# Loading the first modulation tiles into a place of their own, in one queue in the order of need

## The reference, cut to what matters

```python
xc = ctx
for l in range(DEPTH):
    mod = jax.nn.silu(c) @ w_mod[l] + b_mod[l]
    mod_c = jax.nn.silu(c_ctx) @ w_mod[l] + b_mod[l]
    sh1, sc1, g1, sh2, sc2, g2 = jnp.split(mod[:, None, :], 6, axis=-1)
    ...
    h = x * (1 + sc1) + sh1
    hc = xc * (1 + sc1c) + sh1c
    y, yc = _token_mixers(h, hc, w_in[l], ...)
```

## Time and profile before

| | |
|---|---|
| median of 3 runs | 3222.01 us (3219.78 to 3222.47) |
| the profiled execution | 3220.32 us, span of its instructions 3219.0 us |
| granted TensorE clock, mean | 0.966 of full |
| busy: PE, DVE, ACT, POOL | 94%, 44%, 33%, 10% |
| loads from HBM | 294.29 MB, 92 GB/s over the span |

### The profile page before, as it was taken

The page is one execution under the profiler, slowest core; times in us unless marked ns, Lnnn a source line. Parts: engine busy times, 40 slices in busy tenths (PEclk is TensorE's granted clock), DMA queues, the critical chain, the costliest instruction groups (busy, mean ns, idle before and its releaser), DMA issues.

```text
span 3219.0 us, 41567 instructions
## 1 busy us (share of the span) xinstructions
PE 3019.1 (94%) x17128; PEld 2308.4 (72%) x17128; DVE 1418.2 (44%) x2184; ACT 1072.9 (33%) x1807; POOL 313.1 (10%) x334
## 2 busy tenths in 40 slices
PE   5989999999999988999999998997889999899998
PEld 3766657788888866766667776775567888678886
DVE  2556542423233345654444445536734444344443
ACT  3235441412122242553422335212533323342222
POOL 1012220300000030221201002000310000110000
PEclk7999999999999999999999999998989999889999
DMA  6313134222212122103343322422322232222322
GB/s 236 94 58 105 34 119 150 86 99 85 66 60 65 58 77 69 60 14 127 134 150 98 103 87 79 165 94 92 99 85 92 94 96 92 67 66 92 98 92 79
DMA packets 83876, 299.08 MB, mean 93 GB/s; under 512 B 9479, under 2 KB 11783, under 8 KB 83432
## 3 DMA queue, kind: packets, MB, share of 16 engines
q1 hardware_dynamic: 79200, 286.30, 27.2%
q10 hardware_dynamic: 4488, 10.12, 0.9%
HBM read 294.29 MB, written 2.10 MB: 92 GB/s over the span
## 4 chain that ended last, share of the span: by engine, by line
PE 87%; DVE 5%; ACT 4%; issue 2%; DMA 1%; POOL 1%; ACTq 0%; DVEq 0%; POOLq 0%
PE bank L592 42%; PE bank L596 21%; PE bank L1013 4%; PE bank L455 3%; PE bank L1030 3%; PE bank L1074 2%; PE bank L2682 2%; PE bank L1828 1%; PE bank L1566 1%; DMA t<-in_mod 1%; PE bank L1450 1%; PE bank L1022 1%; ACT t L1288 1%; ACT t L843 1%; ACT t L1112 1%
## 5 line engine op out<-in xcount | busy, mean ns | idle before, releaser
L592 PE MATMUL bank<-t 128*128 128x512 f32 (+1 forms) x6432 | 1757.3, 374 | 26.5 <-DVE t L2326 11.1
L592 PEld LDWEIGHTS bank<-t 128*128 128x128 f32 x6432 | 1113.0, 189 | 297.1 <-issue 69.1
L596 PE MATMUL bank<-t 128*128 128x512 f32 (+1 forms) x3216 | 1070.7, 372 | 5.9 <-POOL t L852 5.7
L596 PEld LDWEIGHTS bank<-t 128*128 128x128 f32 x3216 | 556.8, 189 | 127.4 <-POOL t L852 12.0
L486 ACT ACTIVATE t<-t 128x1024 fp32r<-128x1024 f32 x350 | 366.3, 1050 | 558.4 <-PE bank L596 497.5
L496 DVE TENSOR_TENSOR t<-t 128x1024 fp32r<-128x1024 f32 x350 | 430.5, 1234 | 262.4 <-ACT t L486 258.8
L609 DVE SCALAR_TENSOR_TENSOR t<-bank,t 128x512 f32<-128x512 f32 x192 | 129.8, 693 | 511.0 <-PE bank L596 484.2
L933 DVE TENSOR_TENSOR t<-t 128x512 f32<-128x512 f32 (+1 forms) x128 | 98.4, 769 | 335.8 <-ACT t L913 335.8
L913 ACT ACTIVATE t<-bank 128x512 f32<-128x512 f32 (+1 forms) x128 | 83.3, 651 | 418.7 <-PE bank L596 418.7
L1214 POOL TENSOR_SCALAR t<-t 128x768 f32<-128x768 f32 (+3 forms) x160 | 125.7, 788 | 576.3 <-DVE t L1182 576.3
L455 PE MATMUL bank<-t 128*32 128x256 f32 x1536 | 128.9, 414 | 33.7 <-DMA t<-in_mod 23.5
(11 more groups left out here) (289 smaller groups left out, 2281.4 us busy)
## 6 DMA issues: line engine op xcount, KB each, us to landing
t<-in_mod SPq DMA_DIRECT2D x192, 512.0 KB, 4.3
t<-in_l0fc SPq DMA_DIRECT2D x64, 512.0 KB, 3.5
t<-in_l1fc SPq DMA_DIRECT2D x64, 512.0 KB, 3.5
t<-in_s0fc SPq DMA_DIRECT2D x64, 512.0 KB, 3.5
t<-in_s1fc SPq DMA_DIRECT2D x64, 512.0 KB, 3.5
t<-in_mixin SPq DMA_DIRECT2D x24, 512.0 KB, 3.5
t<-in_l0in SPq DMA_DIRECT2D x12, 512.0 KB, 3.6
t<-in_l1in SPq DMA_DIRECT2D x12, 512.0 KB, 3.5
```

The source lines that it names most:

```text
L592: pe.matmul(acc.ap[:, o:o + m], w[:, ws], Hh[:, k, o:o + m], start=k == 0 and w is hi, stop=False)
L596: ins = pe.matmul(acc.ap[:, o:o + m], hi[:, ws], Hl[:, k, o:o + m], start=False, stop=k == NK - 1)
```

## The change

The first 16 modulation tiles get a buffer of their own, `early`, 64 KB in each partition. It is allocated and given back before `mixer_memory` is called, so it lies on the bytes of the first mixer's buffers (`cqh` to `F` and the start of `Hh`), which are written only after `mod_at(0, 1)`. None of the 16 loads waits for PE. The four loads of x move from ACT's queue to SP's and lose their waits. SP's first entries are written out by hand: modulation tiles 0 to 12, dense tiles 0 and 1, the first quarter of x, modulation tiles 13 to 15, the other three quarters of x, dense tiles 2 and 3. From there on the sorted order is as before, with modulation tiles 16 to 18 first. ACT and DVE split two dense tiles, not three, before they make h, and the third after it.

```diff
--- before.py
+++ after.py
@@ -247,7 +247,7 @@
 def first_order(t, l):
     name = f"l{l}"
-    t.tile((name + "in", 3))
+    t.tile((name + "in", 3), 0 if l else 1)
     t.tile((name + "in", 4), 1)
     for i in (5, 6, 7, 8, 0, 1, 2, 9):
         t.fill(1, l + 1)
@@ -364,7 +364,7 @@
     XTt = sb(ctx, [P, NK, T])
     XT = [XTt[:, k, :] for k in range(NK)]
-    NR, NS, NM = 4, 3, 3
+    NR, NS, NM, NE = 4, 3, 3, 16
     modw = sb(ctx, [P, NM, 1024])
     whi = sb(ctx, [P, NS, 1024], F32R)
@@ -418,23 +418,44 @@
     def sp_tiles():
-        first = seq.place[seq.mod_keys[10]]
-        tiles = [(seq.freed_at(seq.keys[i - NR]) if i >= NR else first, seq.place[key], key)
-                 for i, key in enumerate(seq.keys)]
-        mods = [(seq.place[seq.mod_keys[i - NM]] if i >= NM else -1, seq.place[key], key)
-                for i, key in enumerate(seq.mod_keys)]
-        for _, _, key in sorted(tiles + mods, key=lambda x: x[0:2]):
-            if key in seq.index:
-                i = seq.index[key]
-                if i >= NR:
-                    SPQ.wait_ge(*at("pe_tile", i - NR))
-                sp.dma_start(raw[:, i % NR, :], din[key[0]][key[1]]).then_inc(*up(f"tile_in{i % NR}", i, 16))
-            else:
-                i = seq.mods[key]
-                if i >= NM:
-                    SPQ.wait_ge(*at("pe_mod", i - NM))
-                sp.dma_start(modw[:, i % NM, :],
-                             din[f"mod{key[1]}"][NK * key[2] + key[3]]).then_inc(*up(f"mod_in{i % NM}", i, 16))
+
+        for i in range(13):
+            sp_mod(i)
+        sp_tile(0)
+        sp_tile(1)
+        sp_x(0)
+        for i in range(13, NE):
+            sp_mod(i)
+        for j in range(1, 4):
+            sp_x(j)
+        for i in range(2, NR):
+            sp_tile(i)
+        tiles = [(seq.freed_at(seq.keys[i - NR]), seq.place[seq.keys[i]], i, sp_tile) for i in range(NR, len(seq.keys))]
+        mods = [(seq.place[seq.mod_keys[i - NM]] if i >= NE + NM else -1, seq.place[seq.mod_keys[i]], i, sp_mod)
+                for i in range(NE, len(seq.mod_keys))]
+        for _, _, i, send in sorted(tiles + mods, key=lambda x: x[0:2]):
+            send(i)
+
+    def sp_tile(i):
+        key = seq.keys[i]
+        if i >= NR:
+            SPQ.wait_ge(*at("pe_tile", i - NR))
+        sp.dma_start(raw[:, i % NR, :], din[key[0]][key[1]]).then_inc(*up(f"tile_in{i % NR}", i, 16))
+
+    def sp_mod(i):
+        key = seq.mod_keys[i]
+        if i >= NE + NM:
+            SPQ.wait_ge(*at("pe_mod", i - NM))
+        sp.dma_start(mod_place(i), din[f"mod{key[1]}"][NK * key[2] + key[3]]).then_inc(*up(mod_sem(i), i, 16))
+
+    def sp_x(j):
+        sp.dma_start(XTt[:, 2 * j:2 * j + 2, :], din["xT"][:, 2 * j:2 * j + 2, :]).then_inc(*up(f"x_in{j}", 0, 16))
+
+    def mod_place(i):
+        return early[:, i, :] if i < NE else modw[:, (i - NE) % NM, :]
+
+    def mod_sem(i):
+        return f"early_in{i}" if i < NE else f"mod_in{(i - NE) % NM}"
     def pe_weights(key):
         i = seq.index[key]
@@ -450,10 +471,10 @@
                     PEQ.wait_ge(*b7.claim(key[0:3]))
                 i = seq.mods[key]
                 PEQ.wait_ge(*at("dve_cond", L // 2))
-                PEQ.wait_ge(*at(f"mod_in{i % NM}", i))
+                PEQ.wait_ge(*at(mod_sem(i), i))
                 for j in range(4):
                     ins = pe.matmul(b7.ap[32 * j:32 * j + 32, 0:256], cond[:, k, :],
-                                    modw[:, i % NM, 256 * j:256 * j + 256], start=k == 0, stop=k == NK - 1)
+                                    mod_place(i)[:, 256 * j:256 * j + 256], start=k == 0, stop=k == NK - 1)
                 ins.then_inc(*up("pe_mod", i))
             elif key[0] == "turn":
                 _, L, part = key
@@ -536,10 +557,6 @@
         ACTQ.wait_ge(*at("vec_in", 0))
         act.activation(sg, cs, ACT.Exp, scale=-1.0).then_inc(*up("act_own", "silu"))
         ACTQ.wait_ge(*at("pool_eps", 1))
-
-        for j, i in enumerate((1, 3, 5, 6)):
-            ACTQ.wait_ge(*at("pe_mod", i))
-            act.dma_start(XTt[:, 2 * j:2 * j + 2, :], din["xT"][:, 2 * j:2 * j + 2, :]).then_inc(*up(f"x_in{j}", 0, 16))
     def act_rest():
         act.dma_start(tabs[:, :, :], din["tabs"][:, 0:4, :]).then_inc(*up("rest_in", "tabs", 16))
@@ -2859,6 +2876,7 @@
                     ins = act.activation(Hh[:, k, o:o + m], XT[k][:, o:o + m], ACT.Identity, scale=gain(k, i),
                                          bias=shift(k, i))
                 ins.then_inc(*up("act_hhi", ("h0", k)))
+            act_tiles(("l0in", 4))
             for k in range(NK):
                 ACTQ.wait_ge(*at("pool_h", ("h0", k)))
                 ACTQ.wait_ge(*at("dve_h", ("h0", k)))
@@ -2877,6 +2895,7 @@
                 if k:
                     DVEQ.wait_ge(*at("dve_h", ("h0", k - 1)))
                     dve_hlo("h0", k - 1, tmp, Hh, Hl, T)
+            dve_tiles(("l0in", 4))
             dve_rest()
         def pool_first():
@@ -2914,6 +2933,9 @@
     act_prologue()
     dve_prologue()
     pool_prologue()
+
+    with ExitStack() as here:
+        early = sb(here, [P, NE, 1024])
     sp_tiles()
     scope = mixer_memory(T)
     first_h(scope)
```

## The result

The changed kernel took 3206.55 us (median of 5 runs, 3205.12 to 3208.77) where the kernel before took 3221.09 (5 runs, 3218.7 to 3222.47). The ratio is 0.9957, with a 95% interval from 0.9947 to 0.9968: 14.5 us less by the medians, 0.43% faster. The forecast was 3206.6 us and 15.4 us less, counted from 3222.01, the median of the three runs known then.

What follows compares the result with a forecast made beforehand. PE was taken to bound the whole kernel (94% busy), and loads the start. Loads 14.9, tail 0.55 and clock 0 summed to 15.4 us, so 3222.0 - 15.4 = 3206.6 us, range 3202 to 3213.

Steps and rivals of the forecast that it cites:

- What bounds the start: From 9 to 46 us the DMA engines are 94% busy at 344 GB/s, full with bytes not needed yet.
- more in flight can't help much; the order can: At the start, more loads in flight would gain little because the DMA is full; reordering the loads would gain.
- The loads: Prologue: 8.65 MB from the third modulation tile on at 415 GB/s, so tile 15 starts at 29.5, 14.9 us earlier.
- The rival with 344 GB/s: Prologue loads run slower than 415 GB/s, at the mixed stretch's mean: gain 11.1 us, time 3210.9; chance 0.13.
- PE behind the loads: Prologue: a tile lands every 1.26 us and PE takes 1.13 at half clock, so the loads set the time.
- The tail: From tile 15 to the first dense matmul: two splits ahead of h instead of three, gaining 0.55 us.
- The clock: Start of the dense part: half clock expected again after 5 us with hardly any PE work, so 0 us gained.
- The 3.1 us for a start at full clock: If PE entered the dense part at full clock, 3.1 us more; rival at 3203.5 us, chance 0.07.
- `vec` did not starve: Rival: `vec` in ACT's queue lands only after SP's loads, at about 40 us; time 3229 to 3236, chance 0.03.
- The quarters of x behind tile 15: Three loads of x landing at 31.4, 33.3 and 35.2, hidden by 4 us, or by 2 at 344 GB/s.
- given back behind 60 us: Rival: something behind 60 us takes back over 9 us; time about 3217 to 3222, chance 0.07.
- The sum: Whole kernel: 14.9 + 0.55 + 0 = 15.4 us less, from 3222.0 to 3206.6 us, 0.48% faster.

Runs made afterwards that it cites:

- e5: The changed kernel with the loads of modulation tiles 16 and 17 moved ahead of tile 13; 3211.25 us in one run.
- e2: The changed kernel with x's four loads back in ACT's queue with their waits for PE; 0.9983 of the kernel before, 3213.59 us.
- e4: The changed kernel with all 16 modulation tiles loaded ahead of dense tiles 0 and 1 and x; 0.9950 of the kernel before, 3202.31 us.
- e1: The changed kernel with its load order but modulation tiles back in three places, waiting for PE; 0.9986 of the kernel before, 3214.64 us.
- e3: The changed kernel with three dense tiles split ahead of h, as before the change; 3208.83 us in one run.
- e9: The changed kernel unedited, run again beside e10 on one chip; 0.9957 of the kernel before, 3206.80 us.
- e7: The changed kernel with two unused products keeping PE busy before the first dense matmul; 0.9952 of the kernel before, 3205.43 us.
- e8: e4 with dense tiles 0 and 1 split before the wait for the turned part 1; 0.9938 of the kernel before, 3200.94 us.
- e10: e8 with the two idle products of e7 on PE; 0.9932 of the kernel before, 3199.64 us.
- e6: e4 with each modulation load from tile 6 held until PE used the tile six before; 0.9939 of the kernel before, 3200.99 us.
- e11: e4 with modulation tiles 1, 3, 5, 7 and 9 issued by ACT instead of SP; 3200.96 us in one run.

## Why the prediction was right, step by step

**What bounds the start.** Right, and shown: e5 adds 1.05 MB in front and pays 2.84 us, e2 lets x pass and pays 5.8, e4 takes 1.83 MB away from the front of tile 13 and gets 4.2 back at tile 15. The sentence "more in flight can't help much; the order can" was half wrong. In e2 x comes early as before, and with more tiles in flight tile 15 starts 8.1 us earlier; some 5.5 of that are left when the two dense tiles moved behind it are taken off. The order alone gave 7.4 (e1). The 94% busy share over 9 to 46 us hid it: a mean of 344 GB/s isn't the 413 of full engines. The forecast didn't suffer, since it counted the new stretch by its own bytes at the full rate. In that list of bytes not needed yet, "three modulation tiles beyond the 16th" was a misreading too: the load of the second of them was issued at 44.24, when tile 15 had all but landed.

**The loads.** Forecast 14.9 us, measured 13.86. From the third tile to tile 15 it took 22.1 us (8.40 to 30.51) instead of 20.8. Of the 1.3, 0.3 are the rate (8.65 MB at 410 instead of 415 GB/s), the rest is the gap between tiles 12 and 13: 6.75 us where 1.28 and 1.83 MB at 410 GB/s make 5.74. That 1.0 us is a term that the sum didn't have. The trace shows it at dense tile 1, which stands between the two: 15 shares had landed by 23.70 and the last at 24.74, after an instruction packet of 1.08 us at 22.10. `vec` came 0.3 us earlier than before, which gives 0.2 back. The rival with 344 GB/s is out. The Trainium skill's figure of about 358 GB/s as what binds a load from HBM (DMA: Bandwidth & Descriptors, "Where 436 GB/s comes from") doesn't hold for this core: the stretches after say 405 to 413 for over 30 us.

**PE behind the loads.** Right: in the unbroken stream tiles come every 1.28 us and PE stands 0.2 to 0.65 us before each.

**The tail.** Forecast 0.55, measured 0.23 (6.93 to 6.70). DVE's second split ended 2.61 us behind the start of the first, not 2.50, and PE began 0.25 behind it, not 0.05. The term is small, but the step behind it was incomplete: I costed the edit of `hold` by the split alone. e3 shows that in the new order it also covers the load of dense tile 2, worth 3.5 us.

**The clock.** Forecast 0, measured 0.49: the rise came in the second slice, so that two slices took 6.72 us, not 7.21; in e9 they took 6.94. How early the rise comes differs between two profiles of one kernel, so this is no gain of the change. The reason I gave (PE's rest between the parts) is shown by e7. The 3.1 us for a start at full clock were too much: 1.95 in e7 and 2.2 between e8 and e10, or 2.4 to 2.7 with the 0.49 that the changed kernel had already.

**The rivals.** `vec` did not starve: it landed by 5.28 us, with nine loads of SP issued by then. The quarters of x behind tile 15 ended no wait. Nothing of size was given back behind 60 us.

**The sum.** 13.86 + 0.23 + 0.49 = 14.6, against 15.4 forecast. The misses of 1.0 and 0.3 downwards and 0.5 upwards partly cancelled, and the 14.5 of the medians fits the measured terms. That 3206.6 hit 3206.55 is luck: the gain was 0.9 us short, and the kernel before came out 0.9 lower with two more runs (3221.09, not 3222.01). The first dense matmul, which has no such help, was forecast for 35.9 and came at 37.21.

## What to carry to other kernels

When a prologue waits for loads, list the bytes that must land before the step it waits for and divide by the rate of a full stretch; that gives the start to about 1 us, and then take out of the list whatever the tail behind that step can cover (here two weight tiles and a quarter of x, 4.7 us at the first dense matmul). Order and buffers belong together: without buffers the loads wait for the consumer, without order the engines are full of the wrong bytes, and here e1 and e2, each without one of them, gave 7.4 and 8.1 us of the 13.9 (2.6 of the 8.1 by the dense tiles that e2 moves too). When a load moves back in the queue, look for the instructions that read it and stand in program order ahead of the critical one: here a third split ahead of h would have cost 3.5 us.

## What the hardware did that I had not expected

One gap of 1.0 to 1.5 us more than the rest stood in the arrival of the tiles in every kernel whose queue was kept full (2.65 us in e4, 2.53 in e6, 2.66 in e11), while the engines together kept moving about 410 GB/s. After it the tiles came every 1.28 us again, so the delay was never made up. It did not depend on six or sixteen loads ahead, and it did not go with the position in SP's queue. It does go with one packet of instructions. In the changed kernel and e2 to e11 one such packet (16 KB, 1.08 to 1.11 us) starts between 22 and 30 us. In the first or second load to land after it one share of 16 falls 0.96 to 1.59 us behind the others, and it stays behind in the loads that follow. Before the packet, the last share came at most 0.13 us behind the 15th (more only in e2, while x came from a second queue). So one of the 16 engines seems to give that time to the program's instructions, and every tile then waits for that engine. In e1, where the queue runs dry between loads, the packet came at 28.15 and the last share of the next load was 0.72 us late, but of the one after it only 0.19. No run takes the packet away: that it is the cause is argued from the timing alone, and what sets the timing is open.

SP's issue of a load took 0.38 to 0.64 us for the first 13 in the changed kernel, then mostly 1.05 to 1.08 us, with one of 2.98 and one of 4.50. That cost nothing here, since SP had nothing else to do. On ACT such issues hold back compute: the five in e11 took 2.81 us, and PE began at 7.18, where it began at 6.56 in e4, though `vec` landed as early in both (5.15 and 5.14).

The granted clock during the modulation tiles was not the same from run to run: with a tile on PE in each 1.28 us it fell to half near 15 us in the first profile of the changed kernel and held at full until 22 us in the second (e9). That had no effect on the start of tile 15 (30.51 and 30.71), since the loads set the pace.
